# Two-block kernel: gate products of the recurrence in runs of four matmuls at half as many places

## What is computed

```python
pool_l, q_l, k_l, v_l, rw_l, gate_l = split_cols(p_l, IN_SPLITS)   # p_l = modulate(x) @ w_in
...
S_c, y_c = wkv_bidir(S0, *prep_c[:6])      # 256 context tokens, both directions
_, y_l = wkv_bidir(S_c, *prep_l[:6])       # 512 tokens, both directions
rwo_l = rwkv_output(y_l, prep_l, ...)
mix_l = merge_branches((pool, att_l, rwo_l), gate_l, w_br, w_out)  # sigmoid(gate_l) weighs the branches
...
x = x + mod[:, 5] * hier_moe(f_l, *moe_par)  # 32 experts, top 2
```

## Time and profile before

| what | value |
|---|---|
| median of three runs | 1852.87 us |
| time of the profiled execution | 1852.16 us |
| its span | 1850.3 us |
| TensorE busy, of the span | 1683.9 us (91%) |
| VectorE busy | 862.3 us (47%) |
| ScalarE busy | 517.9 us (28%) |
| recurrence, about | 764 to 1203 us of the span |
| expert weights streamed, about | 1281 us to the end |

### The profile page before, as it was taken

The page is one execution under the profiler, slowest core; times in us unless marked ns, Lnnn a source line. Parts: engine busy times, 40 slices in busy tenths (PEclk is TensorE's granted clock), DMA queues, the critical chain, the costliest instruction groups (busy, mean ns, idle before and its releaser), DMA issues.

```text
span 1850.3 us, 36848 instructions
## 1 busy us (share of the span) xinstructions
PE 1683.9 (91%) x16262; PEld 901.6 (49%) x16262; DVE 862.3 (47%) x1563; ACT 517.9 (28%) x995; POOL 115.8 (6%) x145
## 2 busy tenths in 40 slices
PE   5999999999998999999999999998999978777886
PEld 3444555445546555456667766544553323223332
DVE  3887564547647475446565645253361221212110
ACT  3810443311137321554255431131231100101010
POOL 0000100000000000210000000001000110000001
PEclk9999999999999999999999998999999999999999
DMA  9254634331220130232221210375469999999997
GB/s 395 111 173 160 247 125 153 127 122 46 69 90 1 54 123 1 104 110 72 77 82 50 66 55 21 124 292 208 177 254 423 416 425 415 421 414 425 416 424 278
DMA packets 50613, 358.31 MB, mean 194 GB/s; under 512 B 8405, under 2 KB 8621, under 8 KB 30736
## 3 DMA queue, kind: packets, MB, share of 16 engines
q1 hardware_dynamic: 37232, 307.31, 41.4%
q0 software_dynamic: 13216, 48.59, 8.0%
HBM read 336.61 MB, written 27.36 MB: 197 GB/s over the span
## 4 chain that ended last, share of the span: by engine, by line
PE 70%; DMA 18%; ACT 4%; DVE 4%; issue 2%; SPq 1%; POOL 0%; DVEq 0%; ACTq 0%; POOLq 0%
PE psum L210 67%; DMA arena<-in_w 18%; ACT arena L207 3%; PE psum L213 3%; DVE arena L157 1%; DVE arena L167 1%; SPq L143 1%; DVE arena L183 1%; ACT L207 1%; DVE arena L163 0%; DVE arena L171 0%; DVE arena L175 0%; POOL arena L141 0%; DMA arena<-in_tok 0%; DVE arena L162 0%
## 5 line engine op out<-in xcount | busy, mean ns | idle before, releaser
L210 PE MATMUL psum<-arena 32*32 32x16 f32 (+9 forms) x15618 | 1606.6, 303 | 138.9 <-DMA arena<-in_w 66.3
L210 PEld LDWEIGHTS psum<-arena 32*32 32x32 f32 (+5 forms) x15618 | 832.4, 134 | 861.3 <-issue 748.0
L207 ACT ACTIVATE arena<-psum 128x512 f32<-128x512 f32 (+4 forms) x350 | 174.1, 497 | 833.3 <-PE psum L210 631.5
L157 DVE TENSOR_TENSOR arena<-arena,psum 128x512 f32<-128x512 f32 (+3 forms) x124 | 62.1, 501 | 352.4 <-PE psum L210 204.1
L157 DVE TENSOR_TENSOR arena<-arena 128x512 f32<-128x512 f32 (+8 forms) x311 | 188.9, 607 | 32.5 <-ACT arena L207 16.1
L207 ACT ACTIVATE arena<-arena 128x512 f32<-128x512 f32 (+9 forms) x253 | 139.0, 549 | 201.9 <-DVE arena L183 52.3
L207 ACT ACTIVATE arena<-psum,arena 128x128 f32<-128x128 f32 (+3 forms) x221 | 111.6, 505 | 260.6 <-PE psum L213 135.5
L167 DVE SCALAR_TENSOR_TENSOR arena<-arena 128x512 f32<-128x512 f32 (+7 forms) x236 | 158.9, 673 | 27.7 <-DMA arena<-in_w 10.5
L213 PE MATMUL psum<-arena 128*128 128x128 f32 x644 | 103.7, 290 | 19.5 <-ACT arena L207 11.6
L213 PEld LDWEIGHTS psum<-arena 128*128 128x128 f32 x644 | 73.7, 145 | 78.6 <-issue 54.1
L175 DVE RECIPROCAL arena<-arena 128x1 f32<-128x1 f32 (+4 forms) x69 | 78.7, 1141 | 63.9 <-ACT arena L207 60.4
(11 more groups left out here) (50 smaller groups left out, 186.6 us busy)
## 6 DMA issues: line engine op xcount, KB each, us to landing
arena<-in_w SPq DMA_DIRECT2D x117, 2048.0 KB, 42.3
arena<-in_w SPq DMA_DIRECT2D x24, 1024.0 KB, 12.1
arena<-in_w SPq DMA_DIRECT2D x48, 256.0 KB, 3.1
arena<-kd POOLq DMA_DIRECT2D x28, 256.0 KB, 3.4
gd<-arena SPq DMA_DIRECT2D x24, 256.0 KB, 3.6
arena<-gd SPq DMA_DIRECT2D x24, 256.0 KB, 5.3
arena<-in_w SPq DMA_DIRECT2D x8, 512.0 KB, 11.3
arena<-in_w POOLq DMA_DIRECT2D x8, 512.0 KB, 5.0
```

The costliest lines, as they stand in the source:

```text
L157: return self.ends(self.e.tensor_tensor(out, a, b, op))
L207: return self.ends(self.e.activation(out, a, func, **kw))
L210: return self.ends(self.e.matmul(out, lhs, rhs, start=start, stop=stop))
```

## The change

`TENSOR_STEPS` is written anew, nothing else. The steps that are not `gate` keep their order. The 93 pairs stood at 77 places: 68 single pairs, four of two, four of three, one of five. Now they stand at 44: 42 of two pairs (four matmuls), one of four, one of five. At 33 places between two steps there is no gate matmul any more, at three a pair less, and at 36 a pair more, which is the one that stood at the next place. With that each run of two pairs uses one half of a product's weights. The lists of VectorE and ScalarE, the loads and the stores are the same. Two lines of the table:

```diff
-kn1.00 u1.10 x2.00 gate p1.01 kn1.10 x2.10 gate p1.11 u2.00 gate x3.00 gate u3.00 gate x4.00 gate u2.10 u4.00 gate x5.00 gate x3.10 u5.00 gate gate
+kn1.00 u1.10 x2.00 gate gate p1.01 kn1.10 x2.10 p1.11 u2.00 gate gate x3.00 u3.00 gate gate x4.00 u2.10 u4.00 gate gate x5.00 x3.10 u5.00 gate gate
```

More of the change, by code:

```diff
@@ L333 @@
 TENSOR_STEPS = """
-p1.00 p1.10 gate gate gate gate gate g1.00 gate g2.00 gate gate gate g1.10 gv.000 x1.00 a.000 kn0.00 g2.10 gate gate gv.100 u1.00 a.100 x1.10 kn0.10
-kn1.00 u1.10 x2.00 gate p1.01 kn1.10 x2.10 gate p1.11 u2.00 gate x3.00 gate u3.00 gate x4.00 gate u2.10 u4.00 gate x5.00 gate x3.10 u5.00 gate gate
-g1.01 s.000 u3.10 gate m.000 g2.01 gv.001 x4.10 a.001 x1.01 gate u4.10 kn0.01 s.001 u1.01 x5.10 kn1.01 gate u5.10 p1.02 g1.11 s.100 m.001 y.00 g2.11
-x2.01 gate m.100 gv.010 x1.11 a.010 gv.101 kn0.11 a.101 u1.11 u2.01 kn1.11 gate x3.01 p1.12 u3.01 gate x4.01 gate x2.11 gate s.101 u4.01 u2.11 gate
@@ L338 @@
[L338 to L349, removed]
+p1.00 p1.10 gate gate gate gate gate g1.00 gate gate g2.00 gate gate g1.10 gv.000 x1.00 a.000 kn0.00 g2.10 gate gate gv.100 u1.00 a.100 x1.10 kn0.10
@@ new lines @@
+kn1.00 u1.10 x2.00 gate gate p1.01 kn1.10 x2.10 p1.11 u2.00 gate gate x3.00 u3.00 gate gate x4.00 u2.10 u4.00 gate gate x5.00 x3.10 u5.00 gate gate
+g1.01 s.000 u3.10 gate gate m.000 g2.01 gv.001 x4.10 a.001 x1.01 u4.10 kn0.01 s.001 u1.01 x5.10 kn1.01 gate gate u5.10 p1.02 g1.11 s.100 m.001 y.00
+g2.11 x2.01 m.100 gv.010 x1.11 a.010 gv.101 kn0.11 a.101 u1.11 u2.01 kn1.11 gate gate x3.01 p1.12 u3.01 x4.01 gate gate x2.11 s.101 u4.01 u2.11 gate
+gate m.101 x3.11 y.10 x5.01 gv.110 u5.01 a.110 u3.11 gate gate g1.02 s.010 x4.11 gate gate m.010 g2.02 gv.011 u4.11 a.011 x1.02 x5.11 kn0.02 s.011
@@ new lines @@
+gate gate u5.11 u1.02 kn1.02 g1.12 co.02 s.110 m.011 y.01 g2.12 m.110 x2.02 gv.111 gv.020 a.111 a.020 x1.12 kn0.12 s.111 p1.03 u1.12 m.111 y.11 gate
+gate gv.120 u2.02 a.120 x3.02 gate gate u3.02 kn1.12 co.12 x2.12 x4.02 gate gate p1.13 u4.02 u2.12 x5.02 gate gate x3.12 u5.02 g1.03 s.020 u3.12 gate
+gate m.020 g2.03 gate gate gv.021 x1.03 a.021 x4.12 kn0.03 u1.03 s.021 u4.12 kn1.03 co.03 x5.12 x2.03 gate gate u5.12 p1.04 g1.13 s.120 m.021 y.02
+m.120 x1.13 gv.030 u2.03 a.030 u1.13 gv.121 gate gate a.121 x3.03 g2.13 s.121 m.121 y.12 kn0.13 gv.130 kn1.13 a.130 co.13 u3.03 x2.13 gate gate p1.14
@@ new lines @@
+x4.03 u2.13 u4.03 gate gate x3.13 x5.03 u3.13 u5.03 gate gate gate gate g1.04 s.030 x4.13 m.030 g2.04 gate gate u4.13 gv.031 x1.04 a.031 x5.13 kn0.04
+u5.13 s.031 u1.04 g1.14 s.130 kn1.04 co.04 gate gate m.130 x1.14 p1.05 gv.131 u1.14 a.131 m.031 y.03 g2.14 x2.04 gv.040 a.040 s.131 kn0.14 kn1.14
+u2.04 gate gate co.14 m.131 x3.04 y.13 p1.15 u3.04 gv.140 a.140 x4.04 x2.14 gate gate u2.14 u4.04 x5.04 gate gate u5.04 gate gate x3.14 g1.05 u3.14
+s.040 m.040 g2.05 gate gate x4.14 gv.041 u4.14 a.041 x1.05 x5.14 kn0.05 s.041 gate gate u5.14 u1.05 kn1.05 g1.15 s.140 co.05 x2.05 m.041 m.140 g2.15
@@ L350 @@
+y.04 gv.141 x1.15 a.141 kn0.15 gv.050 u1.15 s.141 a.050 kn1.15 co.15 x2.15 u2.05 m.141 x3.05 gate gate u2.15 y.14 x3.15 u3.05 gv.150 f.04 a.150 u3.15
+x4.05 f.14 gate gate x4.15 gate gate u4.15 u4.05 f.04 x5.15 f.14 gate gate u5.15 x5.05 s.150 u5.05 gate gate s.050 m.150 gv.151 m.050 a.151 gate gate
+gv.051 s.151 a.051 s.051 m.151 y.15 end.1 m.051 gate gate y.05 end.0 gate gate
 """
```

## The result

| | before | after |
|---|---|---|
| median of four runs, same chip | 1852.73 us (1851.10 to 1854.57) | 1895.89 us (1890.71 to 1901.33) |
| ratio | | 1.0234, 95% interval 1.0212 to 1.0257 |
| profiled execution, its span | 1852.16, 1850.3 us | 1896.51, 1894.7 us |

The change makes the kernel slower by 43 us. The direction was forecast, the size was not: 1871.7 us was the forecast and 1887 the upper end of its range.

A forecast was written before the change was run, and what follows sets the result against it. TensorE's queue was taken to set the pace in the recurrence. The terms, -6 + 13.1 + 1.7 + 7 + 3 = +18.8 us, gave a forecast median of 1871.7 us, with a range of 1851 to 1887.

The forecast's parts named there:

- First term: Recurrence, 33 vacated places: each gives back 1.9 us while the added pair costs 1.72, together -6 us.
- Second and third terms: Recurrence: +13.1 us of new waits at 18 vacated places with inputs too little early; +1.7 us at `u4.15`.
- What I had costed at nothing: ScalarE's copies of gate results, loads of weight halves and stores: no added time.
- Fourth term: Recurrence: longer stretches without a gate matmul add TensorE "issue" idle time from late code, +7 us, ends 0 and 13.9.
- Fifth term: Recurrence: more pauses bring one more stretch at the lower clock, +3 us; none (0) to three (9 us).
- The carry to the end: Behind the recurrence: TensorE has no idle time and expert weights start after, so its difference reaches the end one for one.
- Supply and clock decide: Rival, recurrence: waits as forecast, issue time doubled, three more lower-clock stretches; +32 us, 1885 us; chance 0.18.
- Drains decide: Rival, recurrence: inputs come early enough, only fewer tile-form switches count; -6 to -9.6 us, say 1845 us; chance 0.12.
- A draw: Rival, recurrence: waits at lower end (6.5 and 1.7), no more issue time or half clock; +2 us, 1855; chance 0.14.

The follow-up runs named there:

- e8_spread2: Before's list in single matmuls, one of a pair moved into long stretches of small matmuls, 15 splits: 1839.20 us, ratio 0.9913 to before.
- e1_ample: Before with only the change's 15 moves away from places where the input had been there over 1.8 us early: ratio 1.0107 to before.
- e10_tight_spread: Before with the change's moves at the 18 places where input was hardly early, plus 14 of e8_spread2's 15 splits: ratio 1.0086 to before.

## Why the prediction was wrong

**First term, -6 us for fewer runs: too large.** By the estimate above the fewer runs gave back some 2 us. In the other direction the price holds: the same working gives 4 us more for the 15 further runs of e8_spread2, 0.27 each.

**Second and third terms, +13.1 and +1.7 us of waits: right.** Waits grew by 13.5 us, where the two make 14.8. Weight loads after, at `x3.00` and `u3.00` and at `u4.15`:

```profile
815.60 0.63 PEld L210 LDWEIGHTS psum<-arena 32*32 32x32 f32 x64 [0.76 <-issue]
816.73 0.95 PEld L210 LDWEIGHTS psum<-arena 32*32 32x32 f32 x66 [0.50 <-DVE arena L157]
...
1208.06 1.82 PEld L210 LDWEIGHTS psum<-arena 32*32 32x32 f32 x128 [5.12 <-DVE arena L157]
```

`u3.00` starts 1.13 us behind `x3.00` with 0.50 us of waiting on VectorE, as forecast (1.1 and 0.5). At 13 of the 18 places the trace shows the step waiting on VectorE or ScalarE now, 0.2 to 1.8 us, some 10 us in sum; `u4.15` waits 5.12 us instead of 2.55, 2.6 more where I had 1.7. The rest are waits at other steps, such as 1.25 us at `u2.00`, which I had put into the upper end alone, so that the sum fits so well is in part luck. What I had costed at nothing stayed so: TensorE waits for no DMA in this stage.

**Fourth term, +7 us of issue: mis-sized.** It measured 11.3, inside the bound of 13.9. I had costed the 15 ample moves at a gain as far as the covers went, and put the price of longer stretches into this term alone; e1_ample shows them costing 20 us, 9.0 of it issue. The Trainium skill (Runtime: NRT & Kernel Launch, section Instruction fetch mechanics) calls the crossing of a code block mostly hidden; with 25.2 us of issue in 478, each long piece of it tied to a packet of code, the trace does not agree.

**Fifth term, "one stretch, +3 us" at the lower clock, with 9 as its bound: this is the step that failed.** Seven more stretches came and 58 us more at the lower level, worth some 25 us. Two things were wrong in it. It looked at the new waits alone ("most of the new waits are shorter than 1.73 us"), though the fourth term had just added issue stops, and ten of the 15 stretches follow an issue stop. And it took the 1.73 us of the earlier trace rows for the least that counts: e10_tight_spread shows the clock falling behind a wait of 0.99 us, and the table above half of the short pauses among small matmuls followed by it. I had one example, though before has 37.5 us of lower clock in this stage and I had looked at 6 of them. The Trainium skill (TensorE: Matmul & The Clock Gate, section A second HAM failure mode: psum-queue depth-cycling) reports of another kernel that frequent short idle times between groups of matmuls make the clock swing between its two levels; the trace agrees in kind, with pauses of 0.5 to 4.3 us ahead of 13 of the 15 stretches. With the measured sizes the sum is -2 + 13.5 + 11.3 + 25 = 47.8 us, against 48.5 at `y.05`; the first and the last of these are estimates.

**The carry to the end: right.** SyncE's queue of expert weights, after:

```profile
1327.26 524.86 SPq L143 DMA_DIRECT2D arena<-in_w  x101
```

It starts 45.9 us later than in the earlier trace rows, and the span is 44.4 us longer.

**The rivals.** "Supply and clock decide" named the right pieces and gave the clock 9 us where it cost some 25, so it fell 11 us short of the median. "Drains decide" is refuted from the other side: e8_spread2 has 15 runs more than before and is 16 us faster. "A draw" had 8.2 us of waits and no more issue time or half clock; all three grew by more.

## What to carry to other kernels

Large matmuls between small steps did three things here beside their own work: they covered the round trip of the step ahead, they broke up stretches in which TensorE uses up its code fastest, and a short pause right behind them seldom brought the clock down. Before taking one away, price the first two, and then price the clock on top: add up the time at the lower clock over the whole stage, not at one example, and take it to grow with the pauses of both sorts. In an engine-bound stage full of small tiles it paid to cut the large work finer (0.29 us for each further run) and to put it where the trace shows issue idle time.

## What the hardware showed that was not expected

TensorE's clock fell behind short pauses: behind a wait of 0.99 us in e10_tight_spread, whose profiled execution has 71.7 us at the lower level in a stage with 32 us of pauses in all. And code came too late for an engine that is busy 91% of the span: 153 stops of over 0.5 us in thirteen traces, each ending 1.2 to 1.6 us behind a packet of code. The time at the lower clock varies between executions: e10_tight_spread's seven runs lie between 1857.78 and 1877.71 us, and on that chip before itself between 1844.39 and 1859.58, so a difference of one stretch needs the trace and can't be read from the times.
